# Score matmuls of a hybrid attention layer: the order of 128-row and 64-row matmuls where a step has two banks

## What is computed

```python
# A, for each block i of 128 queries
sc = einsum('bthcd,bshcd->bhcts', qb, k) * scale        # c = 0, 1: two maps
sc = where(key_pos <= q_pos, sc, NEG_INF); p = softmax(sc)
a = p[:, :, 0] - lam * p[:, :, 1];  out = einsum('bhts,bshe->bthe', a, v)
# B, for each block of 128 queries, keys of this block and the one before
sc = einsum('bntkgd,bnskd->bnkgts', qb, k_band) * scale
sc = where(in_window & (key_abs >= 0), sc, NEG_INF)
p = softmax(concatenate([sc, sink]))[..., :-1];  o = einsum('bnkgts,bnskd->bntkgd', p, v_band)
# then gates, output projection w_out, residual
```

## Time and profile before

| | |
|---|---|
| median of 3 runs | 1970.88 us (1969.64 to 1972.56) |
| span of the profiled execution | 1968.6 us; its own time is not listed apart from the three above |
| instructions | 27876 |
| PE busy | 1916.5 us, 97% |
| VectorE (DVE) busy | 1114.6 us, 57% |
| ScalarE (ACT) busy | 800.1 us, 41% |
| GpSimd (POOL) busy | 434.7 us, 22% |
| HBM traffic | 93 GB/s over the span |

### The profile page before, as it was taken

The page is one execution under the profiler, slowest core; times in us unless marked ns, Lnnn a source line. Parts: engine busy times, 40 slices in busy tenths (PEclk is TensorE's granted clock), DMA queues, the critical chain, the costliest instruction groups (busy, mean ns, idle before and its releaser), DMA issues.

```text
span 1968.6 us, 27876 instructions
## 1 busy us (share of the span) xinstructions
PE 1916.5 (97%) x8920; PEld 1521.5 (77%) x8920; DVE 1114.6 (57%) x2255; ACT 800.1 (41%) x2116; POOL 434.7 (22%) x662
## 2 busy tenths in 40 slices
PE   3999999999999999999999999999999899999999
PEld 3788777777777777777777777787777677788887
DVE  6733565655656556565565666757667767333333
ACT  5412344444444444444444444434444544222221
POOL 6511221312213122131221312213223431100000
PEclk7999999999999999999999999999999999999999
DMA  5122222222222213222232222322223533444445
GB/s 198 38 79 76 69 81 69 69 80 60 85 70 68 79 58 88 70 68 79 59 87 70 69 80 64 102 76 74 85 83 90 189 112 111 142 166 139 157 146 173
DMA packets 256505, 184.97 MB, mean 94 GB/s; under 512 B 31137, under 2 KB 227745, under 8 KB 255393
## 3 DMA queue, kind: packets, MB, share of 16 engines
q1 hardware_dynamic: 254352, 183.85, 30.7%
q10 hardware_dynamic: 2064, 0.01, 0.1%
HBM read 138.71 MB, written 45.09 MB: 93 GB/s over the span
## 4 chain that ended last, share of the span: by engine, by line
PE 88%; DVE 4%; DMA 2%; issue 2%; ACT 2%; POOL 1%; SPq 1%; DVEq 0%; ACTq 0%
PE ps_a L854 20%; PE ps_a L856 20%; PE ps_a L855 20%; PE ps_a L898 5%; PE ps_a L897 4%; PE ps_b L940 3%; PE ps_b L955 3%; PE ps_b L855 2%; PE ps_b L856 2%; PE ps_b L854 2%; PE ps_b L891 2%; PE ps_b L986 1%; DMA qkv_sb<-qkv_a_dram 1%; PE ps_b L957 1%; DVE stage_rows L1125 1%
## 5 line engine op out<-in xcount | busy, mean ns | idle before, releaser
L854 PE MATMUL ps_a<-hT_hi,w_hi_sb 128*128 128x512 f32 x1696 | 693.3, 409 | 6.5 <-DVE stage_rows L1209 4.3
L856 PE MATMUL ps_a<-hT_hi,w_lo_sb 128*128 128x512 f32 x1696 | 666.3, 393 | 0.0
L855 PE MATMUL ps_a<-hT_lo,w_hi_sb 128*128 128x512 f32 x1696 | 663.5, 391 | 0.0
L1125 DVE TENSOR_TENSOR w_lo_sb<-w_raw_sb,w_hi_sb 128x512 fp32r<-128x512 f32 (+1 forms) x320 | 228.2, 716 | 274.0 <-ACT w_hi_sb L657 271.8
L856 PEld LDWEIGHTS ps_a<-hT_hi,w_lo_sb 128*128 128x128 f32 x1696 | 319.7, 189 | 71.6
L854 PEld LDWEIGHTS ps_a<-hT_hi,w_hi_sb 128*128 128x128 f32 x1696 | 320.8, 189 | 69.8 <-issue 7.3
L855 PEld LDWEIGHTS ps_a<-hT_lo,w_hi_sb 128*128 128x128 f32 x1696 | 321.1, 189 | 58.1
L657 ACT ACTIVATE w_hi_sb<-w_raw_sb 128x512 fp32r<-128x512 f32 (+1 forms) x320 | 197.9, 621 | 227.3 <-DMA w_raw_sb<-in_w_out 100.3
L749 ACT ACTIVATE attention_parts<-ps_b 128x512 fp32r<-128x512 f32 (+3 forms) x160 | 76.9, 521 | 308.6 <-PE ps_b L940 308.6
L1125 DVE TENSOR_TENSOR ps_a<-ps_a,mask 128x128 f32<-128x128 f32 (+2 forms) x192 | 80.3, 419 | 214.7 <-PE ps_a L898 214.0
L817 ACT ACTIVATE expd<-ps_a,neg_max 128x256 f32<-128x256 f32 (+7 forms) x128 | 95.1, 743 | 212.9 <-DVE neg_max L1266 212.5
(11 more groups left out here) (125 smaller groups left out, 2700.7 us busy)
## 6 DMA issues: line engine op xcount, KB each, us to landing
w_raw_sb<-in_w_in SPq DMA_DIRECT2D x200, 256.0 KB, 3.1
w_raw_sb<-in_w_out SPq DMA_DIRECT2D x104, 256.0 KB, 3.1
qkv_a_dram<-stage_rows SPq DMA_DIRECT2D x48, 256.0 KB, 2.4
qkv_sb<-qkv_a_dram SPq DMA_DIRECT2D x64, 192.0 KB, 2.9
x_raw_sb<-in_x SPq DMA_DIRECT2D x8, 1024.0 KB, 6.3
gates_dram<-stage_rows SPq DMA_DIRECT2D x32, 256.0 KB, 2.5
gate_y<-gates_dram SPq DMA_DIRECT2D x128, 64.0 KB, 2.4
y_dram<-gate_y SPq DMA_DIRECT2D x128, 64.0 KB, 2.2
```

The lines of the kernel that those rows point to most:

```text
L854: pe.matmul(dst, a_hi, b_hi, start=start, stop=False)
L855: pe.matmul(dst, a_hi, b_lo, start=False, stop=False)
L856: return pe.matmul(dst, a_lo, b_hi, start=False, stop=stop)
L1125: return dve.tensor_tensor(o, a, b, op)
```

## The change

`q_times_k` is gone. `scores_a` first issues the 128-row matmuls of all its spans and then the 64-row ones. `scores_b` takes its four heads in two pairs; a pair `p` has one head in each bank and in each half of the rows, and its two 128-row matmuls come first, then its two 64-row ones. `s_done` is raised after the two 64-row matmuls of the second pair, once for each. The operands, the number of matmuls and their sums are the same.

```diff
--- before.py
+++ after.py
@@ -891,12 +891,6 @@
                     mm = pe.transpose(p_tr[bank][:, r * P:(r + 1) * P], stage[:, b, r * P:(r + 1) * P], ident[:, :])
                 mm.then_inc(sm["tp_done"], 1)
 
-            def q_times_k(dst, q, k, h, k_lo):
-
-
-                pe.matmul(dst, q, k, start=True, stop=False)
-                return pe.matmul(dst, q[h, :], k_lo, start=False, stop=True)
-
             def scores_a(st, c, it, first):
                 i = st["i"]
                 w = (i + 1) * P
@@ -906,9 +900,12 @@
                 wait(pe, sm["x_done"], st["G"] * 2 + c)
                 flat = p_s.rearrange("p a b -> p (a b)")
                 h = slice(c * HD, (c + 1) * HD)
-                for lo in range(0, w, 512):
-                    t = slice(lo, min(w, lo + 512))
-                    mm = q_times_k(flat[:, t], q_pair[:, c * P:(c + 1) * P], k_dup[c][:, t], h, kT_lo[h, t])
+                q = q_pair[:, c * P:(c + 1) * P]
+                spans = [slice(lo, min(w, lo + 512)) for lo in range(0, w, 512)]
+                for t in spans:
+                    pe.matmul(flat[:, t], q, k_dup[c][:, t], start=True, stop=False)
+                for t in spans:
+                    mm = pe.matmul(flat[:, t], q[h, :], kT_lo[h, t], start=False, stop=True)
                 mm.then_inc(sm["s_done"], 1)
 
             def scores_b(st, it, first):
@@ -917,12 +914,15 @@
                 wait(pe, sm["x_done"], st["G"] * 2)
                 t = slice(max(i - 1, 0) * P, (i + 1) * P)
                 lo = P if i == 0 else 0
-                for r in range(2):
-                    h = slice(r * HD, (r + 1) * HD)
-                    for p in range(2):
-                        mm = q_times_k(p_s[:, r, p * 256 + lo:p * 256 + 256],
-                                       q_pair[:, (2 * r + p) * P:(2 * r + p + 1) * P], k_dup[0][:, t], h, kT_lo[h, t])
-                    mm.then_inc(sm["s_done"], 1)
+                for p in range(2):
+                    dst = [p_s[:, r, p * 256 + lo:p * 256 + 256] for r in range(2)]
+                    q = [q_pair[:, (2 * r + p) * P:(2 * r + p + 1) * P] for r in range(2)]
+                    for r in range(2):
+                        pe.matmul(dst[r], q[r], k_dup[0][:, t], start=True, stop=False)
+                    for r, h in enumerate(half_rows):
+                        mm = pe.matmul(dst[r], q[r][h, :], kT_lo[h, t], start=False, stop=True)
+                        if p:
+                            mm.then_inc(sm["s_done"], 1)
 
             def turn_probs(st, it, first):
                 i = st["i"]
```

## The result

The changed kernel takes 1924.04 us (1922.37 to 1924.51, 4 runs) against 1971.14 us for the kernel before on the same chip: ratio 0.976, 95% interval 0.9746 to 0.9774. That is 47.1 us less. Forecast were 1925.7 us and a range of 1918 to 1941 us. The sum came out within 2 us by luck: as the traces show, two of its terms were off in opposite directions by nearly the same amount.

What follows compares the result with a forecast made beforehand. TensorE's own stream was taken as the bound nearly everywhere. Savings of 25.6 (A) and 24.2 (B) less 3.0 and 1.6 given back make 45.2 us: 1970.9 to 1925.7 us, range 1918 to 1941 us.

Steps and rivals of the forecast that it cites:

- The price of a change of rows: Each TensorE change between 128 and 64 rows costs 0.20 us: 0.11 running out, 0.11 bare load; 0.43 against 0.23.
- A, 25.6 us: Mixer A, blocks 4 to 7: 64 calls with two banks, each 0.40 us shorter (1.60 to 1.21).
- The unseen step: Two 64-row matmuls in a row: taken as the 128-row case, 0.23 us at 512 columns; upper bound 0.43 us.
- The first three rivals: Load bare in one half (0.16, 1932.7 us), between all 64-row matmuls (0.07, about 1939.8), or full change (0.04, 1948).
- B, 24.2 us: Mixer B: 32 two-bank calls, 2.39 to 1.63 us; 28 save 0.76 us, 4 save 0.74; nothing for halves side by side.
- Given back at the turn of the output, 1.6 us: In A the output's turn waits for a bank DVE's copy releases: about 0.2 us, once in each of 8 units.
- Given back where DVE is the bound, 3.0 us: Four calls of B lie at DVE-bound places (1544 to 1590, 1623 us); their 4 x 0.75 us is nearly all lost.
- Slack in B's odd steps, nothing: In B, DVE gains 0.26 us where TensorE gains 0.76; 0.5 us of slack go, and no loss was counted.
- PEld's idle time before the 64-row loads: Sign expected in the profile: idle time falls from 65.5 to about 39 us, since 128 of 320 loads are hidden.
- The slower rival: No change saved and B's first bank released late, masks 0.39 us later: up to 12.5 us, 1983 us; chance 0.02.
- that of no effect: The order changes nothing, since the cost belongs to each 64-row matmul: 1970.9 us; chance 0.02.
- The signs of being wrong: 64-row matmuls 0.32 us or more apart, new TensorE waits at lines 940, 968, 897, or clock under 1.00, 200 to 1500 us.

## Why the prediction was right, and where its terms were not

- **What bounds the kernel**: right. Most of what TensorE's stream lost came out at the end, 47.1 of 56.3 us.
- **The price of a change of rows, 0.20 us**: right for the changes that the new order takes away (0.39 us for two in A). With no change left, calls and the matmuls behind them are 0.16 to 0.19 us shorter for each change of before in the usual forms of call, a little less than the price. The reading of the earlier trace rows that was to confirm it doesn't: PEld's idle time before a 64-row load is 0.24 us in A and 0.15 us in B, it depends on the matmul before, and only the mean is 0.20 us.
- **A, 25.6 us**: measured 24.9 us; the full call 1.20 us for 1.21.
- **The unseen step** (a load between two 64-row matmuls of one half is hidden): right, the load starts at 303.35 us under the matmul from 303.24 us. The first three rivals, which kept 0.11 or 0.20 us at this place, fall. The Trainium skill's sentence that loads overlap matmuls in flight "only when row_grp differs" (TensorE: Matmul & The Clock Gate, Part 3) doesn't hold here, in the 64-row mode either.
- **B, 24.2 us**: wrong, measured 31.4 us. The step that failed is "So I take nothing for two halves of the rows that could work side by side". It argued from the pace of loads on 128 rows, 0.106 us each, that the loads would set the pace anyway. But two loads into different halves also run at once: the pair started 0.003 us apart, took 0.32 us, and took 0.43 us as soon as both were put on the same half. The Trainium skill has it: matmuls on distinct row groups run concurrently, about 4 ns apart (TensorE: Matmul & The Clock Gate, Part 3). The trace agrees. The prediction had used that page for a rival and passed by this line.
- **Given back at the turn of the output, 1.6 us**: the mechanism was right, the size was not: 4.3 us in nine places. The step that was off is that DVE "doesn't move with the 0.40 us of the call just before": it doesn't move with the call before that one either, so TensorE comes 0.75 us early against DVE's copy and not 0.40. The forecast also counted idle time alone (0.2, found 0.29), where behind a wait the matmul before has run out and the load lies bare, 0.16 us more. The ninth place is at the passage to B.
- **Given back where DVE is the bound, 3.0 us**: measured 6.2 us. It counted the saving of four calls as the forecast had it, 0.75 us each; each saved 1.0 us, and with that its count makes 3.9. Another 1.5 us is the slow clock behind the wait of line 940, which was not there before. The remaining 0.8 us is open, and that the waits belong to these four calls and no others isn't shown.
- **Slack in B's odd steps, nothing**: right. Between 1190 and 1540 us only one longer interval, by 0.49 us, appeared, the ninth turn.
- **PEld's idle time before the 64-row loads** was to fall from 65.5 to about 39 us; it is 32.8 us before line 908 and 8.0 us before line 923, 40.8 together.
- **The slower rival and that of no effect** fall: the calls got shorter in both mixers, no wait of TensorE grew by more than 1.5 us, and both masks of the call shown were done 2.78 us after its start (1357.42) where it had been 3.20.
- **The signs of being wrong**: one of them, "a pace of 0.32 or more between the two 64-row matmuls", contradicts the prediction's own working, which has 0.34 us at this place; 0.34 was measured, and a bare load would have made it 0.43. The others didn't appear: the granted clock was 1.00 from 200 to 1500 us, and the wait at line 940 had been there before and only grew.

So the mechanism held and the closeness of the sum was luck: 7.2 us too little in B stood against 5.9 us too little given back and 0.7 us too much in A (45.2 + 7.2 - 5.9 - 0.7 = 45.8 us).

## What to carry to other kernels

Where small matmuls on part of the rows stand between full ones, count the changes, not the matmuls: each costs what it takes the one before to run out and the next load to lie bare, here 0.16 to 0.20 us. Group them by mode, put neighbours on different halves of the rows (here also on different banks), or fill the missing rows with zeros if they are free; the last gave twice the gain of reordering. When a stream of one engine is shortened locally, look for a wait with less slack than the saving. Follow the other engine's chain back to its start and count every shortened piece that lies beside it, here two calls in 12 us and not one. Price the wait with the drain and the bare load behind it.

## What the runs showed that I had not expected

- Two 64-row matmuls on different halves and banks, with their loads, ran in the time of one: 0.32 us for the pair against 0.43 us on the same half.
- Four of them in two pairs took 0.44 us (1320.18 to 1320.62 us), so the loads of the next pair hide under the pair in flight.
- A lone 64-row matmul isn't shorter than a 128-row one: with its load hidden and its end to run out, one of 512 columns took 0.32 us either way (302.70 to 303.24 us is 0.23 + 0.32 at 128 rows, 303.24 to 303.90 us 0.34 + 0.32 at 64), so filling up the rows with zeros costs TensorE nothing there.
- Two ScalarE copies a block, 78 us of busy time in all, cost no time that can be told (0.9523 with them, 0.9533 without), with ScalarE busy for 47% of the span.
- A wait that grew from 1.03 to 2.45 us cost TensorE twice: by itself, and by 1.5 us of lower granted clock behind it.
